# Expert blocks of 160 rows, stationary rows and plain fp32 weights, in a decoder layer with a mixture of experts

## The reference, cut to what matters here

```python
def swiglu(x, w_gate, w_up, w_down):
    return (jax.nn.silu(x @ w_gate) * (x @ w_up)) @ w_down

def moe(x, lp):                       # x: (1104, 1024)
    scores = jax.nn.sigmoid(x @ lp['router_w'])            # 64 experts
    _, idx = lax.top_k(scores + lp['router_bias'], 8)
    gate = take_along_axis(scores, idx); gate = gate / sum(gate) * 2.5
    # tokens grouped by expert; each expert: gate and up (1024, 256), down (256, 1024)
    routed = sum over the 8 chosen experts of gate * swiglu(x, w_g[e], w_u[e], w_d[e])
    return routed + swiglu(x, lp['w_sh_gate'], lp['w_sh_up'], lp['w_sh_down'])
```

## Time and profile before

| what | value |
|---|---|
| median of three executions | 2700.27 us |
| the profiled execution: time, span | 2703.4, 2701.4 us |
| PE busy | 2435.6 us, 90% of the span |
| PE weight loads busy | 1812.3 us, 67% |
| DVE, ACT, GpSimd busy | 1306.9 (48%), 1050.7 (39%), 663.4 (25%) |
| mean granted clock of TensorE | 0.95 of full speed |
| queue 1 (SyncE's DMAs) | 269.06 MB |
| queue 0 (GpSimd's DMAs) | 124.70 MB |

### The profile page before, as it was taken

One profiled execution on the slowest core, in us unless ns is written; L12 is line 12 of the kernel. 1 busy time (PEld: TensorE's weight loads), 2 busy tenths in 40 slices (PEclk: granted clock), 3 DMA queues, 4 the chain that ended last, 5 costly groups with the idle time before them and its releaser, 6 DMA issues. The chain is left out here.

```text
span 2701.4 us, 39475 instructions
## 1 busy us (share of the span) xinstructions
PE 2435.6 (90%) x14550; PEld 1812.3 (67%) x14550; DVE 1306.9 (48%) x2582; ACT 1050.7 (39%) x1706; POOL 663.4 (25%) x574
## 2 busy tenths in 40 slices
PE   7899799899967799999995789999999999999990
PEld 4456566564356466665553378899898998999980
DVE  0544355100176001011662267777777777777764
ACT  1055433100142000000120056666666666666652
POOL 0022321000041000000243024444444444434433
PEclk9989999899978899999997989999999999999995
DMA  3000043200010401001130399999999999999964
GB/s 135 0 12 2 17 175 124 98 32 0 2 35 2 169 31 47 23 23 45 32 113 27 112 291 281 282 288 287 279 283 281 288 284 280 284 286 288 287 163 160
DMA packets 113772, 394.95 MB, mean 146 GB/s; under 512 B 41590, under 2 KB 51142, under 8 KB 85254
## 3 DMA queue, kind: packets, MB, share of 16 engines
q1 hardware_dynamic: 78390, 269.06, 28.4%
q0 software_dynamic: 35296, 124.70, 18.7%
HBM read 325.16 MB, written 69.13 MB: 146 GB/s over the span
## 5 line engine op out<-in xcount | busy, mean ns | idle before, releaser
L2128 PE MATMUL banks<-split 128*128 128x384 f32 x1792 | 538.3, 363 | 0.0
L2242 DVE TENSOR_TENSOR split<-rest,split 128x2048 fp32r<-128x2048 f32 x192 | 438.9, 2286 | 113.3 <-ACT split L2186 113.3
L2126 PE MATMUL banks<-split 128*128 128x192 f32 x2048 | 482.8, 256 | 0.0
L2148 PE MATMUL banks<-split 128*128 128x512 f32 x1536 | 406.6, 407 | 17.5 <-ACT rest L2199 13.6
L2126 PEld LDWEIGHTS banks<-split 128*128 128x128 f32 x2048 | 389.2, 192 | 2.7
L2186 ACT CAST split<-rest 128x2048 fp32r<-128x2048 f32 x192 | 359.2, 1904 | 65.8 <-DMA rest<-in_w_exp_gate 60.8
L1587 PE MATMUL banks<-big 128*128 128x368 f32 x1152 | 358.4, 474 | 14.8 <-DMA big<-in_w_merge 14.8
L2076 POOL DMA_INDIRECT y_rows<-rest x128 | 263.8, 2061 | 340.2 <-ACT rest L2199 299.9
L2128 PEld LDWEIGHTS banks<-split 128*128 128x128 f32 x1792 | 338.9, 189 | 0.0
L2148 PEld LDWEIGHTS banks<-split 128*128 128x128 f32 x1536 | 276.2, 190 | 73.0 <-ACT rest L2199 17.5
L1587 PEld LDWEIGHTS banks<-big 128*128 128x128 f32 x1152 | 219.9, 191 | 153.0 <-issue 16.6
(11 more groups left out here) (338 smaller groups left out, 3036.9 us busy)
## 6 DMA issues: line engine op xcount, KB each, us to landing
rest<-in_w_exp_gate SPq DMA_DIRECT2D x64, 1024.0 KB, 9.0
rest<-in_w_exp_up SPq DMA_DIRECT2D x64, 1024.0 KB, 6.8
rest<-in_w_exp_down SPq DMA_DIRECT2D x64, 1024.0 KB, 7.5
big<-in_w_merge SPq DMA_DIRECT2D x8, 1536.0 KB, 6.7
big<-in_w_cols SPq DMA_DIRECT2D x11, 512.0 KB, 3.3
x_rows<-big SPq DMA_DIRECT2D x9, 512.0 KB, 11.9
y_rows<-big SPq DMA_DIRECT2D x9, 512.0 KB, 2.6
big<-in_x_cols SPq DMA_DIRECT2D x3, 1472.0 KB, 17.2
```

What stands on the lines that cost most here:

```text
L2126: ins = pe.matmul(PS[:, banks[f], 0:CAP], wr[:, s, j, LO, at:at + 128], x[:, k, 0:2], start=False, stop=False)
L2128: ins = pe.matmul(PS[:, banks[f], 0:2 * CAP], wr[:, s, j, HI, at:at + 128], x[:, k], start=False, stop=(k == KD - 1))
L2148: ins = pe.matmul(PS[:, DBANK[c]], hr[:, a, f, HALF * hf:HALF * hf + 128], wr[:, s, DOWN, b, at:at + 512], start=(f == 0 and j == 0), stop ...
L2242: dve.tensor_tensor(wr[:, s, j, LO], raw[:, s, j], wr[:, s, j, HI].bitcast(F32), ALU.subtract).then_inc(parted[j], 1)
```

## The change

It rewrites `stage_experts` and touches what feeds it.

- `CAP` is 160, a main part of 128 slots and a rest of 32.
- The split is gone: no high and low parts, no `split` tensor. All products are plain fp32 from the loaded weights.
- The gathered rows are now the stationary side of gate and up too: 8 main products of 512 columns, gate and up side by side, and for the 32 rest rows 32 products of 128 columns whose outputs go to four partition groups of one bank (`RBANK`). Hidden values [rows, 256] are multiplied by the gate value and transposed on PE (`turn_h`). Down: 4 main products of 512 columns, and 8 of 256 columns for the rest rows in four partition groups.
- PE's order in step n is: gate and up of block n+1, transposes of block n+2, down of block n, the transposes of h of block n+1.
- The entries are loaded three times (gi, wi, si), in 7 DMAs for a block instead of 2; SyncE's order is new (below).
- Gathers and scatters have a bounds check: entries of 1104 and more move no row. The padding rows of `x1_rows` and `y_rows` are gone, with the writes that filled them.
- In the prompt attention the 49 copies are made one by one after each diagonal.

```diff
-CAP = 192
-HALF = CAP // 2
+CAP = 160
...
+        def pick(w):
+
+            if w < 8:
+                p, e = w // 2, w % 2
+                c = TAIL + NEW * w
+                own.link(pool.tensor_copy(S.qs_c[:, p, 64 * e:64 * (e + 1)].rearrange("p (h t) -> p h t", h=HEADS), S.qlat[:, :, c:c + NEW]))
...
         for w in range(U):
             pool.wait_ge(rinv_ready, w + 1)
             if w >= 4:
                 pool.wait_ge(o_full, (w - 4) // 2 + 1)
             pool.tensor_scalar(diag[:, w % 4], S.ident, sums[:, w:w + 1], None, ALU.mult).then_inc(diag_ready, 1)
...
+            pool.wait_ge(diag_ready, w + 1)
+            pick(w)
...
-
-        sp.dma_start(S.x1_dram[T:T + 128], S.x1[:, 0]).then_inc(x1_out, 16)
-        sp.dma_start(S.x1_dram[T + 128:T + CAP], S.x1[0:CAP - 128, 1]).then_inc(x1_out, 16)
-        sp.wait_ge(x1_out, 16 * (NT + 2))
+        sp.wait_ge(x1_out, 16 * NT)
...
             return sp.value_load(S.blocks_i[0:1, 0, bass.ds(n, 1)], min_val=0, max_val=EXPERTS - 1)
 
-        def entries(dst, sems, s, first):
-            sp.dma_start(dst[0:HALF, s].rearrange("p (h w) -> p h w", h=2).bitcast(I32),
-                         S.table[bass.ds(first, CAP)].rearrange("(h p) w -> p h w", p=HALF)).then_inc(sems[s], 16)
+        def entries(dst, sems, s, first, twice=False):
+            src = S.table[bass.ds(first, CAP)]
+            sp.dma_start(dst[:, s, 0:2].bitcast(I32), src[0:MAIN]).then_inc(sems[s], 16)
+            for j in range(2 if twice else 1):
+                sp.dma_start(dst[REST * j:REST * (j + 1), s, 2:4].bitcast(I32), src[MAIN:CAP]).then_inc(sems[s], 16)
...
         with sp.Fori(0, last) as it:
             first = [first_slot(2 * it + s) for s in range(4)]
-            e = [expert(2 * it + 2 + s) for s in range(2)]
+            e = [expert(2 * it + 1 + s) for s in range(3)]
             for s in range(2):
                 n = 2 * it + s
+                sp.wait_ge(main_full, n + 1)
+                weights(s, GATE, e[s + 1])
+                weights(s, UP, e[s + 1])
                 sp.wait_ge(xg_in[s], 32 * (it + 1))
                 entries(gi, gi_in, s, first[2 + s])
-                for j in range(3):
-                    sp.wait_ge(parted[j], n + 1)
-                    weights(s, j, e[s])
                 sp.wait_ge(si_free[s], it + 1)
                 entries(si, si_in, s, first[s])
+                sp.wait_ge(h_made, 2 * n + 2)
+                entries(wi, wi_in, s, first[2 + s], True)
+                sp.wait_ge(part_copied, 3 * n + 3)
+                weights(1 - s, DOWN, e[s])
...
         def gather(s, turn):
-            pool.wait_ge(gi_in[s], 16 * (turn + 1))
+            pool.wait_ge(gi_in[s], 32 * (turn + 1))
             pool.sem_inc(passed, 1)
-            for hf in range(2):
-                pool.indirect_dma_start(out=xg[0:HALF, s, hf], out_offset=None, in_=S.x1_dram,
-                                        in_offset=bass.IndirectOffsetOnAxis(ap=gi[0:HALF, s, 2 * hf:2 * hf + 1].bitcast(I32), axis=0)
-                                        ).then_inc(xg_in[s], 16)
-
-        def scatter(s, turn):
-            if s:
-                pool.wait_ge(y_out[0], 32 * (turn + 1))
-                pool.sem_inc(si_free[0], 1)
-            pool.wait_ge(part_copied, 4 * (2 * turn + s) + 8)
+            for hf, p in enumerate((MAIN, REST)):
+                pool.indirect_dma_start(out=xg[0:p, s, hf], out_offset=None, in_=S.x1_dram,
+                                        in_offset=bass.IndirectOffsetOnAxis(ap=gi[0:p, s, 2 * hf:2 * hf + 1].bitcast(I32), axis=0),
+                                        bounds_check=T - 1, oob_is_err=False).then_inc(xg_in[s], 16)
+
+        def scatter(s, turn, first=False):
+            if s or not first:
+                pool.wait_ge(y_out[1 - s], 32 * (turn + s))
+            pool.sem_inc(si_free[1 - s], 1)
+            pool.wait_ge(part_copied, 3 * (2 * turn + s) + 6)
             pool.sem_inc(passed, 1)
-            for hf in range(2):
-                pool.indirect_dma_start(out=S.y_dram, in_=y[0:HALF, s, hf], in_offset=None, compute_op=ALU.add,
-                                        out_offset=bass.IndirectOffsetOnAxis(ap=si[0:HALF, s, 2 * hf:2 * hf + 1].bitcast(I32), axis=0)
-                                        ).then_inc(y_out[s], 16)
-
-        def body(it, ends):
+            for hf, p in enumerate((MAIN, REST)):
+                pool.indirect_dma_start(out=S.y_dram, in_=y[0:p, s, hf], in_offset=None, compute_op=ALU.add,
+                                        out_offset=bass.IndirectOffsetOnAxis(ap=si[0:p, s, 2 * hf:2 * hf + 1].bitcast(I32), axis=0),
+                                        bounds_check=T - 1, oob_is_err=False).then_inc(y_out[s], 16)
+
+        def body(it, more, first=False):
             for s in range(2):
-                if not ends:
-                    pool.wait_ge(xr_full, 4 * (2 * it + s + 1))
-                    gather(s, it + 1)
-                scatter(s, it)
-            pool.wait_ge(y_out[1], 32 * (it + 1))
-            pool.sem_inc(si_free[1], 1)
-
-        for s in range(2):
-            pool.sem_inc(si_free[s], 1)
+                if s < more:
+                    pool.wait_ge(x_full, 2 * (2 * it + s + 2))
+                    gather(*ahead(s, it, 3))
+                scatter(s, it, first)
+
...
         def gate_up(s, turn_):
...
-                    elif f == 1:
-                        ins.then_inc(gate_full, 1)
-
-        def down(s, turn_, p, f):
+            pe.wait_ge(xrest_copied, n + 1)
+            for j in (GATE, UP):
+                pe.wait_ge(raw_in[j][s], 16 * (turn_ + 1))
+            for k in range(KD):
+                for w in (GATE, UP):
+                    for f in range(2):
+                        q, at = REST * (2 * w + f), DEXP * k + 128 * f
+                        ins = pe.matmul(PS[q:q + REST, RBANK, 0:128], x_rest[:, k], raw[:, s, w, at:at + 128],
+                                        start=(k == 0), stop=(k == KD - 1), skip_group_check=True)
+            ins.then_inc(rest_full, 1)
+            for r in range(2):
+                pe.wait_ge(x_copied[r], n + 1)
+            for k in range(KD):
+                ins = pe.matmul(PS[:, MBANK].rearrange("p (j n) -> p j n", j=2), x_main[:, k],
+                                raw[:, s, GATE:UP + 1, DEXP * k:DEXP * (k + 1)], start=(k == 0), stop=(k == KD - 1))
+            ins.then_inc(main_full, 1)
+
+        def turn_h(s, turn_):
+            pe.wait_ge(h_made, 2 * (2 * turn_ + s) + 2)
+            for f in range(2):
+                pe.transpose(PS[:, HBANK, MAIN * f:MAIN * (f + 1)], h[:, 128 * f:128 * (f + 1)], S.ident)
+            pe.transpose(PS[:, HBANK, 2 * MAIN:2 * MAIN + 2 * REST], h_rest[0:2 * REST], S.ident[0:2 * REST, 0:2 * REST]).then_inc(hT_full, 1)
...
+            if c == 0:
+                pe.wait_ge(raw_in[DOWN][s], 16 * (turn_ + 1))
+                for g in range(2):
+                    pe.wait_ge(hT_copied[g], n + 1)
+            pe.wait_ge(part_copied, 3 * n + 2 * c + 1)
+            for f in range(2):
+                at = DM * f + 512 * c
+                ins = pe.matmul(PS[:, DBANK[c]], hT_main[:, f], raw[:, s, DOWN, at:at + 512], start=(f == 0), stop=(f == 1))
+            ins.then_inc(part_full, 1)
+
+        def down_rest(s, turn_, following):
+
+            n = 2 * turn_ + s
+            pe.wait_ge(part_copied, 3 * n + 2)
+            if following:
+                pe.wait_ge(xrest_copied, n + 3)
+            for f in range(2):
+                for q in range(4):
+                    at = DM * f + 256 * q
+                    ins = pe.matmul(PS[REST * q:REST * (q + 1), EBANK, 0:256], hT_rest[:, f], raw[:, s, DOWN, at:at + 256],
+                                    start=(f == 0), stop=(f == 1), skip_group_check=True)
+            ins.then_inc(part_full, 1)
...
+                one, two = ahead(s, it, 1), ahead(s, it, 2)
+                if not (ends and s):
+                    gate_up(*one)
+                if not ends:
+                    turn(*two, 0, before=2 * it + s)
+                    turn_rest(*two)
+                    turn(*two, 1)
+                down(s, it, 0)
+                down_rest(s, it, not ends)
+                down(s, it, 1)
+                if not (ends and s):
+                    turn_h(*one)
...
+        def part(s, turn_, c):
+
+            act.wait_ge(part_full, 3 * (2 * turn_ + s) + 2 * c + 1)
+            act.copy(y[:, s, 0, 512 * c:512 * (c + 1)], PS[:, DBANK[c]]).then_inc(part_copied, 1)
+
+        def part_rest(s, turn_):
+
+            act.wait_ge(part_full, 3 * (2 * turn_ + s) + 2)
+            for q in range(4):
+                ins = act.copy(y[0:REST, s, 1, 256 * q:256 * (q + 1)], PS[REST * q:REST * (q + 1), EBANK, 0:256])
+            ins.then_inc(part_copied, 1)
...
+                one, two = ahead(s, it, 1), ahead(s, it, 2)
+                if not (ends and s):
+                    sigmoid_rest(*one)
+                    sigmoid_main(*one)
```

(104 more changed lines are left out.)

244 lines of the change are left out of this document (105 added, 139 removed).

## The result

The changed kernel takes 2906.8 us (median of four executions, 2901.8 to 2911.3) where the kernel before takes 2702.1 beside it: ratio 1.075, 95% interval 1.0715 to 1.0785. It is slower, 2930 was forecast. The profiled execution took 2902.97 us, span 2901.1.

What follows compares the result with a forecast made beforehand. The prediction took a loop of gi tables, GpSimd and SyncE's queue to bound the expert stage at 19.0 us a block; PE's end moved +242, scatter -4, attention -8.7: +229 on 2703.4, 2933, so 2930; range 2770 to 3040.

Steps and rivals of the forecast that it cites:

- PE's step: PE's work for one block of the expert stage: 14.84 us, including 0.2 for changes between strips and full array.
- the ring: Expert stage: loop from one gi landing to the next, through GpSimd and SyncE's queue, sets the period at 19.0 us.
- rival 1: Expert stage: small tables pass the weights, or SyncE's chain is otherwise short, so PE bounds; 2660 us, chance 0.13.
- (a): Part of the ring on GpSimd: it wakes and issues two gathers, 2.7 us.
- (b): Part of the ring on SyncE: it issues two si, three wi, then down, 2.8 us.
- (c): Part of the ring on the weights' queue: down, then gate and up behind it, land in 10.7 us.
- the share of queue 0: Part of the ring: queue 0 moves 138 scattered rows at the same time, adding 1.2 us (0 to 2.4).
- (d): Part of the ring on the weights' queue: gi lands behind the weights, 1.9 us.
- `main_full`: PE's signal in the expert stage: comes some 3.5 us before SyncE asks, so no part of the ring.
- Order of landings: On the weights' queue: all landings followed came in the order of issue; gi landing early would remove the ring.
- Clock: Expert stage: PE's idle stretch lets its clock fall, costing 1.7 us a block; a rival above 3040 us, chance 0.05.
- The sum: Whole kernel: gi(2) at 1580.5, 1266 us of loops, PE's end 2876.5, attention -8.7; profiled 2933, median 2930.

Runs made afterwards that it cites:

- tables-first kernel: The changed kernel with gi issued ahead of gate and up instead of behind them: 2728.2 us, ratio 1.0074 to the kernel before.
- the register loads: The changed kernel with five of SyncE's seven register loads moved behind gate, up and gi: 2893.6 us, ratio 1.0672 to the kernel before.
- the early release: The changed kernel with GpSimd giving si_free before it waits for the next gather's table: 2803.7 us, ratio 1.0344 to the kernel before.

## Why the prediction was right, and where it was off

- **Blocks**: 70, as counted.
- **PE's step**: 14.84 forecast, 15.64 measured. From start to start: turns 1.63 (forecast 1.31), down 4.64 (4.33), h 0.51 (0.33), rest of gate and up 1.89 (1.74), main 6.97 (6.93). The long products were right; the short groups each lasted about 0.1 us longer than their columns. Ten groups of different shape follow one another in a step, so 0.2 for all changes was the mis-sized term, 1.0 is near. That is worked out from the groups' starts; no run took the changes of shape away. The Trainium skill's remark in TensorEngine Tiling (Array Packing), Key Properties, that a change of tiling mode drains the engine, had been priced at 0.06 us; here it and the other changes of shape together come to 0.1 each, and the trace does not tell them apart. It made no difference under the ring, and 56 us where PE bounds: rival 1 said 2660 and the tables-first kernel came to 2728, and 0.80 x 70 = 56 of the 68 between them come from this term.
- **DMA load**: 13.9 us a block forecast. Queue 1 and queue 0 in the 800 us, to set against the earlier trace rows, are below: (0.485 + 0.26) x 18.45 = 13.7. Right; it came close to the bound once the ring and a part of PE's work were gone.

```profile
q1 hardware_dynamic: 45945, 135.58, 48.5%
q0 software_dynamic: 16704, 49.03, 26.0%
```

- **The ring**: found in its place, 18.45 for 19.0; the mechanism is right, and that the number lies so near is partly luck, as terms wrong in both directions partly cancel. (a) 2.7 forecast, 1.5 measured (0.86 + 0.64): SyncE's first table is issued 0.64 us after the first gather's start, when the second gather has not begun (it starts 1.36 us after the first), so GpSimd's increment, which the code puts behind both, passes while their issues are still running; I had put them in a row. (b) 2.8, measured 2.7 and 2.5. (c) and the share of queue 0 11.9, measured 13.2 from down's issue to up's landing in the rounds without the hole. (d) 1.9, measured 0.35 from up's landing to the last table's. So (c), (d) and the share together 13.8, measured 13.6 (0.69 + 1.81 + 11.11), and 15.1 in the rounds with the hole. The hole was missing from the sum; it costs 1.3 a pair, as most of it lies under down's landing.
- **PE in the ring**: 14.8 of 19 us busy were foreseen, and 4.2 idle. The trace has PE busy 0.92 of the time and idle 1.6 us a block, because its step is 0.8 longer than forecast and the low clock stretches it by some 1.25.
- **`main_full`** comes before SyncE asks: 3.5 us forecast. PE's turn began at 2108.14, right behind the last product of gate and up, and gate was issued at 2111.86, 3.7 later, but that round has the hole. Over the 64 rounds gate is issued 3.4 us after the end of that product where there is a hole, and only 1.5 where there is none, in six of 31 rounds less than 0.5. It is no part of the ring, as said, but closer to it than forecast: shorten the ring from the other side and `main_full` is there, as the register loads and the early release show.
- **Order of landings**: I had seen all land in the order of their issues. In the changed kernel the profile gives the `gi` table of 2112.99, issued 0.7 us behind up, 6.5 us to land, 1.9 us before up had landed (9.1 after 2112.31), but this isn't a table that passed the weights. Both tables of a pair count on one semaphore, 32 increments, and the profile takes the first 16 for the first table. In all 64 rounds the increments of the two tables follow those of up two by two, 0.16 to 0.42 us behind, and the last one comes 0.31 to 0.41 us after up's last. The Trainium skill says in DMA: Bandwidth & Descriptors, Queues, rings and completion order, that completion is not in order per issuing engine; none of these landings shows a table that was complete before the weights ahead of it.
- **Clock**: a wait of 5.35 us cost PE 3.6 us at half clock, where 1.7 was said, twice too little. It fell less often than once a block, 19 times in the 43 blocks from 1700 to 2500, and lies within the wait for the ring.
- **The sum**: gi(2) let its gather go at 1572.9, for 1571.8 (1580.5 - 8.7). From there to the last gather 1233.1 for 1266: all of the miss, 33 us. From the last gather (2806.04) to PE's end (2836.6) 30.6 for 30.0; from there to the end of the span 64.5 for 63.1. Attention 9.4 for 8.7. So 2903 for 2933.
- **DVE's port**: the gathers' issues went from a mean of 1331 ns to 1001, as forecast. In the trace of before the 60 issues that overlap a subtraction of L2242 last 1670 ns in the mean, the other 68 1033. That agrees with the Trainium skill, SBUF — State Buffer, SBUF: two separate sides, by which GpSimd cannot write descriptors while DVE runs two-port operations; no run takes L2242 away alone, and the number of rows of a gather changed too.

## What to carry to other kernels

When each engine's work has been costed, follow every small transfer once round: whom does it wake, what does that free, and what stands ahead of it in its queue the next time. Tables of 1 KB and less behind 3 MB of weights, with the issue of the next weights hanging on the tables' user, cost 180 us here, and two lines in another order took it back. To know whether an engine bounds, take work from it: some 2 us less a block for PE gave nothing under the ring and 1.6 without it. And when a forecast comes near, check its terms one by one: here several were off, in both directions, and cancelled.

## What the runs showed that I had not expected

- Seven register loads on SyncE make a hole of 5.2 us at the head of each pair (5.77 less 0.60), which no busy time or wait of the profile shows; one sees it only as the distance between two issues. Five of them moved away took 3.1 us of it.
- Now and then the gather follows the landing of its tables after 2.3 us instead of 0.86: the gather of 2124.07 started 2.3 us after the last table had landed at 2121.8, in two of 64 rounds. Its cause stays open; no run was made for it.
- The expert stage's first gather lay between 1537 and 1553 us in the traces of kernels that are the same up to there. Differences of 10 us in the total should be read only between kernels on one chip.
